# Retention's first two projections issued inside attention's last head, and its raw queries and keys read from other bank pairs

## The chip, the cores and the metric

The kernel runs on one core of a Trainium2 chip. Its time is the device time of one execution in microseconds (us). It is one program of 72862 instructions on five engines: PE (TensorE, matmuls), DVE (VectorE), ACT (ScalarE), POOL (GpSimd) and SP (SyncE, which issues the DMAs). Each engine runs its own instructions strictly in the order in which they are written; engines meet at semaphores only.

## The reference, cut to what matters

Two blocks follow each other on a sequence of 1024 tokens of width 1024. The second block has two layers, and the change is in both. Each layer is

```
h = rmsnorm(x); proj = h @ w_in                  # columns aq, ak, av, ag, bq, bk, bv, bg, cu, cg
o_a = diff_attention(aq, ak, av) * silu(ag)      # 4 heads, two softmax maps each, 8 query blocks of 128
o_b = retention(bq, bk, bv) * silu(bg)           # 4 heads, rotary on bq and bk first
o_c = multiscale_pool(cu) * silu(cg)
x   = x + concat(o_a, o_b, o_c) @ w_out
rotary(t): t1, t2 = halves of t; [t1*cos - t2*sin, t1*sin + t2*cos]
```

The first block (RG-LRU with HGRN2, then RWKV-7) is not touched.

## The kernel before

**Projections.** `h` lies turned in SBUF as two fp16 parts, `u_hi` and `u_lo`; the weights come in units of 1024 x 128, split into `w_hi` and `w_lo`, in a ring of four slots. A product is three matmuls (hi x hi, hi x lo, lo x hi) for each of eight tiles of 128 rows. `channel_major` (L128) gives 128 channels by 1024 tokens: 2 halves x 8 tiles x 3 = 48 matmuls of 128x512 into two PSUM banks. `token_major` (L148) gives the transposed form in 192 matmuls of 128x128. PSUM has 8 banks; `bank_pair(n)` is banks 2n and 2n+1. A slot's round is tracked by `stage_full` (weights landed), `w_half` and `w_full` (split), `w_free` (last matmul of the unit done; the same semaphore tells ACT that the unit's result may be read).

**Attention** (`diff_attention`, once for each layer) runs 32 steps `s`: four heads of eight query blocks. The order is written out by hand. In step `s` PE issues the logits of step `s+2` (12 matmuls, L2287, into banks 0 to 3), turns the attention map of step `s` in two halves (L2301, bank 4), multiplies it with the values in two halves (L2315, bank 5), and between these it issues four *pieces*: a quarter each of one half of a projection of the next head (L2259, L2265, banks 6 and 7). The last head, steps 24 to 31, has no next head, so its pieces are empty. DVE in step `s` adds the bias to the logits of `s+2` and takes their maximum (L2475, twice), combines the two maps of step `s+1` (L2485 to L2492), and then takes what the last piece left in PSUM (`low`, L2460 and L2465). ACT in step `s` first evicts the projection half of the step before (L2370 to L2379), copies the first turned half out (`take_turned`, L2390), does the two exponentials of `s+2` (L2384), and every fourth step takes the finished output (`take_values`, L2397 and L2398) before it copies the second turned half. A norm (L2325) follows on PE two steps behind, its tail (L2403 to L2506) on ACT and DVE. The semaphore `taken[half]` counts the projection halves that were taken out of bank 6 (half 0) or 7 (half 1); its sixteenth count belongs to the gate of the last head. For half 1 that is done in step 24, by ACT and then by DVE after `combine(25)`. POOL splits the weights of retention's four units in the last head; SP has loaded them before.

**Retention** is a block of its own behind it: all engines begin it together when the block before has ended on all. SP loads nine constants (L2612), then weights. PE projects units 0, 1, 2 (queries and keys of head pairs) into bank pairs 0, 1, 2; `cross(n)` (L2627, 2 fp32 matmuls, each two records in a profile) swaps the rotary halves of a raw tile; unit 3 goes to pair 3; `double(0)` (L2640), `cross(2)`, then the values of head 0 (L157). ACT begins with the softplus of twelve decay numbers (L314), which waits for a DVE operation behind the constants, and then, `take_raw` (L2728), evicts each unit and splits the high part of the next weights of that slot (L109). DVE finishes the softplus (L323 to L2789), splits low parts (L115) and rotates (L2799 to L2803, three operations for each raw tile).

Of the kernel before, what the change touches and what calls it, by code (L numbers as in the profile page):

```python
# [20 lines left out]
KT = D // P  # L21
TT = S // P
HALF = 512
# [107 lines left out]
def channel_major(pe, K, slot, rnd, u_hi, u_lo, banks, tile_ready=None):  # L131

    pe.wait_ge(K.w_full[slot], rnd + 2)
    w_hi = K.w_hi[:, slot, :].rearrange("p (k c) -> p k c", k=KT)
    w_lo = K.w_lo[:, slot, :].rearrange("p (k c) -> p k c", k=KT)
    for half, bank in enumerate(banks):
        cols = slice(half * HALF, (half + 1) * HALF)
        for k in range(KT):
            if half == 0 and tile_ready is not None:
                pe.wait_ge(tile_ready, k + 1)  # L140
            for n, (w, u) in enumerate(((w_hi, u_hi), (w_hi, u_lo), (w_lo, u_hi))):
                last = pe.matmul(K.psum[:, bank, :], w[:, k, :], u[:, k, cols],  # L142
                                 start=(k == 0 and n == 0), stop=(k == KT - 1 and n == 2))
    last.then_inc(K.w_free[slot], 1)


def token_major(pe, K, slot, rnd, u_hi, u_lo, banks):
# [163 lines left out]
def small_softplus_scalar(act, x_ready, y_ready, x, y):  # L311

    act.wait_ge(x_ready, 1)
    act.activation(y, x, ACT.Abs)  # L314
    act.drain()
    act.activation(y, y, ACT.Exp, scale=-1.0).then_inc(y_ready, 1)
# [1854 lines left out]
def diff_attention(nc, K, A, tag, layer, first_round, ahead):  # L2171

    H, NQ = A_HEADS, TT
    N = H * NQ
    lam_init = 0.8 - 0.6 * float(np.exp(-0.3 * layer))
    with nc.cleanup_on_exit(), ExitStack() as c:
# [6 lines left out]
        q, k = ([split(late_slots[n][:, a, :]) for n in range(2)] for a in range(2))  # L2183
# [25 lines left out]
        def unit_of(s):  # L2209

            h, j = divmod(s, NQ)
            return (h + 1, j // 2, j % 2) if 0 <= s and h + 1 < H else None
# [8 lines left out]
        with nc.Block() as block:  # L2221
# [21 lines left out]
            def _(pe):  # L2243
# [77 lines left out]
                def norm(part, s):  # L2321

                    pe.wait_ge(o_taken, part + 1)
                    pe.wait_ge(turned_ready, 2 * s + 2)
                    pe.matmul(K.psum[:, T_BANK, :], K.ones[:, :], sq[:, cols(part % 2)], start=True,  # L2325
                              stop=True).then_inc(norm_done, 1)

                def piece(s, n):
                    unit = unit_of(s)
                    if unit:  # L2330
                        project(*unit, n)

                whole(0)
                whole(1)
# [4 lines left out]
                for s in range(N):  # L2339
# [12 lines left out]
                    if part is not None:  # L2352
                        norm(part, s)
                values(N - 1, 1)
                norm(2 * H - 1, N - 1)

            @block.scalar
            def _(act):
# [188 lines left out]
def retention(nc, K, A, tag, layer, first_round, ahead):  # L2547
# [7 lines left out]
    H = B_HEADS  # L2555
    w_in = A["w_in_2"][layer].rearrange("(k p) c -> p k c", p=P)
    with nc.cleanup_on_exit(), ExitStack() as c:
# [37 lines left out]
        chunks = lambda x: x.rearrange("p (c t) -> p c t", c=TT)  # L2595
        cols = lambda half: slice(half * HALF, (half + 1) * HALF)

        SWAP_PAIR = (0, 1, 3, 3)
        slot_of = lambda hd, n: (2 * (hd % 2) + n, first_round + 1 + hd // 2)

        with nc.Block() as block:
# [16 lines left out]
            @block.tensor  # L2618
            def _(pe):
                def cross(n):  # L2620

                    i, a = divmod(n, 2)
                    pe.wait_ge(raw_ready, 4 if n == 2 else n + 1)
                    if n == 3:
                        pe.wait_ge(swap_taken, 3)
                    for half in range(2):
                        last = pe.matmul(K.psum[:, 2 * SWAP_PAIR[n] + half, :], swap[:, :],  # L2627
                                         rot[a][:, i, cols(half)], start=True, stop=True)
                    last.then_inc(swapped, 1)

                def double(hd):
                    i, b = divmod(hd, 2)
                    pe.wait_ge(rotated, 2 * i + 2)
                    if hd:
                        pe.wait_ge(scores_taken, hd)
                    else:
                        pe.wait_ge(raw_ready, 3)
                    for n in range(2):
                        for half in range(2):
                            last = pe.matmul(K.psum[:, 2 + 2 * n + half, :], twice[:, b, :],  # L2640
                                             rot[n][:, i, cols(half)], start=True, stop=True)
                        last.then_inc(doubled, 1)

                def values(hd):
                    if hd:
                        pe.wait_ge(g_taken, hd)
                    else:
                        pe.wait_ge(swap_taken, 1)
                    token_major(pe, K, *slot_of(hd, 0), K.u_hi, K.u_lo, (0, 1))

                def score(hd):
                    i, b = divmod(hd, 2)
                    rows = slice(64 * b, 64 * b + 64)
                    pe.wait_ge(qk2_ready, 2 * hd + 2)
                    for ch in range(TT):
                        toks = slice(ch * P, (ch + 1) * P)
                        last = pe.matmul(chunks(K.bank_pair(1))[:, ch, :], rot[1][rows, i, toks], rot[0][rows, i, toks],
                                         start=True, stop=True)
                    last.then_inc(scores_done, 1)

                def turn(hd):
                    for ch in range(TT):
                        last = pe.transpose(chunks(K.bank_pair(2))[:, ch, :], qk2[:, 1, ch * P:(ch + 1) * P],
                                            K.ident[:, :])
                    last.then_inc(k2_done, 1)

                def delta(hd):
                    pe.wait_ge(k2_ready, hd + 1)
                    pe.wait_ge(v_ready, hd + 1)
                    if hd:  # L2670
                        pe.wait_ge(norm_taken, hd)
                    else:
                        pe.wait_ge(swap_taken, 4)
                    for ch in range(TT):
                        last = pe.matmul(chunks(OUT)[:, ch, :], k2_turned[:, ch, :], v[:, ch, :],
                                         start=True, stop=True)
                    last.then_inc(delta_done, 1)

                def output(hd):
                    pe.wait_ge(scores_taken, hd + 1)  # L2680
                    pe.wait_ge(state_ready, hd + 1)
                    for ch in range(TT):
                        pe.matmul(chunks(OUT)[:, ch, :], v[:, ch, :], scores[:, ch, :], start=True, stop=False)
                        last = pe.matmul(chunks(OUT)[:, ch, :], state[:, ch, :], qk2[:, 0, ch * P:(ch + 1) * P],
                                         start=False, stop=True)
                    last.then_inc(out_done, 1)

                def norm(hd):
                    pe.wait_ge(o_taken, hd + 1)
                    for half in range(2):  # L2690
                        last = pe.matmul(K.psum[:, 6 + half, :], K.ones[:, :], sq[:, cols(half)],
                                         start=True, stop=True)
                    last.then_inc(norm_done, 1)

                for n in range(3):
                    channel_major(pe, K, n, first_round, K.u_hi, K.u_lo, (2 * n, 2 * n + 1))
                pe.wait_ge(consts_in, 16 * 9)
                cross(0)
                cross(1)
                channel_major(pe, K, 3, first_round, K.u_hi, K.u_lo, (6, 7))  # L2700
                for hd in range(H):
                    double(hd)
                    if hd == 0:
                        cross(2)
                    values(hd)
                    if hd:
                        norm(hd - 1)
                    score(hd)
                    turn(hd)
                    if hd == 0:  # L2710
                        cross(3)
                    delta(hd)
                    channel_major(pe, K, *slot_of(hd, 1), K.u_hi, K.u_lo, (0, 1))
                    output(hd)
                norm(H - 1)
# [5 lines left out]
            @block.scalar  # L2721
            def _(act):
                act.preload_act_table_set("natural_log_exp_and_others")
                small_softplus_scalar(act, logit_ready, y_ready, neg_logit[:, :], y[:, :])

                def take_raw(n):
                    unit_done(act, K, n, first_round)
                    act.mul(rot[n % 2][:, n // 2, :], K.bank_pair(n),  # L2728
                            UNSCALE * (KEY_SCALE if n % 2 else 1.0)).then_inc(raw_ready, 1)
                    split_high(act, K, n, first_round + 1)  # L2730

# [16 lines left out]
                    act.wait_ge(m_ready, hd + 1)  # L2748
                    act.mul(K.m_hi[:, hd + H, :], O[:, :], U_SCALE).then_inc(hi_ready, 1)

                for n in range(3):
                    take_raw(n)
                act.wait_ge(gamma_ready, 1)
                decays(0)
                take_raw(3)
# [416 lines left out]
```

## Time and profile before

| what | us |
|---|---|
| median of 3 runs | 3684.61 (3682.11 to 3686.03) |
| the profiled execution | 3681.23 |
| its span, first to last instruction | 3679.2 |
| first layer: attention's last head, then retention up to head 0's values | 2367.9 to 2429.5, to 2481.5 |
| second layer: the same | 3165.6 to 3227.6, to 3279.9 |

Times in rows are microseconds from the start of the span. The clock in a row is the mean granted TensorE clock of the stretch as a share of 2.4 GHz: 1.00 is that, 0.50 is 1.2 GHz.

### The profile page before, as it was taken

The numbers are of one execution on the slowest core, as the hardware profiler recorded it, in microseconds if no ns is written. First come the engines' busy times: TensorE is split into PE (matmuls) and PEld (weight loads), VectorE is DVE, ScalarE is ACT, GpSimd is POOL, SyncE is SP. The second block draws the span as 40 slices with busy tenths as digits, with TensorE's granted clock in tenths as the row PEclk, the third lists the DMA queues.
The fourth block names the chain that finished last, engine by engine and source line by source line (L and its number), as shares of the span: only waits on it lengthen the run. The fifth ranks groups of instructions, "written<-read, shape, count | busy, mean of one in ns | idle before, by whom it ended". The sixth has DMA issues, their size and how long they took to land. (4 is left out here: it accounts for less than half of the span.)

```text
span 3679.2 us, 72862 instructions
## 1 busy us (share of the span) xinstructions
PE 3348.3 (91%) x32106; PEld 2085.2 (57%) x32106; DVE 1877.1 (51%) x2548; ACT 1406.7 (38%) x2026; POOL 551.2 (15%) x350
## 2 busy tenths in 40 slices
PE   6987999978979898999998899989889999899889
PEld 3334666663434343999996466647434566657334
DVE  4654566662253833666663566644352366633442
ACT  3553444442354632333332445533211355523211
POOL 3000000002000001333331133200150232100330
PEclk9998999979989999999999999999999999999999
DMA  5101110104035643111113111020120211020211
GB/s 166 34 23 50 30 40 29 40 0 149 1 107 118 153 115 114 64 64 64 63 45 105 52 46 40 2 62 24 39 82 27 66 38 35 1 68 18 62 62 46
DMA packets 308329, 215.24 MB, mean 59 GB/s; under 512 B 125411, under 2 KB 283950, under 8 KB 305454
## 3 DMA queue, kind: packets, MB, share of 16 engines
q1 hardware_dynamic: 307608, 210.70, 19.2%
q8 instruction: 230, 3.77, 0.4%
q10 hardware_dynamic: 442, 0.37, 0.0%
q14 instruction: 49, 0.40, 0.0%
HBM read 173.26 MB, written 41.98 MB: 59 GB/s over the span
## 5 line engine op out<-in xcount | busy, mean ns | idle before, releaser
L142 PE MATMUL psum<-u,w_hi 128*128 128x512 f16 x2816 | 855.8, 386 | 103.1 <-DVEq L798 32.0
L142 PE MATMUL psum<-u,w_lo 128*128 128x512 f16 x1408 | 542.4, 385 | 0.0
L142 PEld LDWEIGHTS psum<-u,w_hi 128*128 128x128 f16 x2816 | 279.1, 100 | 452.4 <-issue 55.6
L97 POOL TENSOR_TENSOR w_hi<-stage,w_scale 128x1024 f16<-128x1024 f32 x52 | 99.4, 1912 | 1244.8 <-PE psum L142 600.0
L1063 PE MATMUL psum<-w_hi,merged 128*128 128x512 f16 x768 | 236.1, 389 | 24.9 <-PEq L2887 9.1
L115 DVE SCALAR_TENSOR_TENSOR w_lo<-stage,w_hi 128x1024 f16<-128x1024 f32 x124 | 149.3, 1220 | 186.1 <-ACT w_hi L109 186.0
L2475 DVE CUSTOM_DVE_ANT_0 probs_att<-psum,bias_att 128x1024 f32<-128x1024 f32 x128 | 156.8, 1225 | 167.8 <-PE psum L2287 167.6
L142 PEld LDWEIGHTS psum<-u,w_lo 128*128 128x128 f16 x1408 | 139.8, 99 | 172.8 <-issue 11.9
L2265 PE MATMUL psum<-u,w_hi 128*128 128x512 f16 x768 | 231.6, 383 | 6.3 <-PEq L966 6.3
L1063 PE MATMUL psum<-held_hi_out,merged 128*128 128x512 f16 x768 | 231.0, 379 | 0.0
L157 PE MATMUL psum<-w_hi,u 128*128 128x128 f16 x2048 | 173.2, 219 | 0.0
L157 PE MATMUL psum<-w_lo,u 128*128 128x128 f16 x1024 | 172.3, 219 | 0.0
L142 PE MATMUL psum<-mix_b_rp,w_hi 128*128 128x512 f16 x512 | 153.6, 382 | 11.9 <-DVE mix_b_rp L1569 11.4
L157 PEld LDWEIGHTS psum<-w_hi,u 128*128 128x128 f16 x2048 | 158.0, 98 | 4.9 <-issue 4.6
L2384 ACT ACTIVATE probs_att<-probs_att,neg_max_att 128x1024 f32<-128x1024 f32 x128 | 146.3, 1146 | 19.5 <-DVE neg_max_att L2479 19.4
L2315 PE MATMUL psum<-turned_att,merged 128*128 128x128 f32 x1024 | 139.7, 281 | 15.0 <-ACT sq_att L2398 14.6
L2099 DVE COPY_PREDICATED Tt_rc<-tmask_rc,psum 128x256 f32<-128x256 uint32 x192 | 83.6, 444 | 131.9 <-PE psum L1789 110.9
L1063 PE MATMUL psum<-w_lo,merged 128*128 128x512 f16 x384 | 149.4, 389 | 0.0
L2315 PEld LDWEIGHTS psum<-turned_att,merged 128*128 128x128 f32 x1024 | 132.2, 195 | 27.7 <-issue 17.7
L109 ACT ACTIVATE w_hi<-stage 128x1024 f16<-128x1024 f32 x124 | 127.6, 1048 | 53.2 <-PE psum L1063 42.3
L1063 PEld LDWEIGHTS psum<-w_hi,merged 128*128 128x128 f16 x768 | 76.6, 100 | 124.4 <-issue 38.3
L2265 PE MATMUL psum<-u,w_lo 128*128 128x512 f16 x384 | 146.9, 382 | 0.0
(444 smaller groups left out, 6804.8 us busy)
## 6 DMA issues: line engine op xcount, KB each, us to landing
stage<-w_in SPq DMA_DIRECT2D x72, 512.0 KB, 4.0
X<-rwkv_chunks SPq DMA_DIRECT2D x14, 1792.0 KB, 8.0
stage<-ab_w_in SPq DMA_DIRECT2D x48, 512.0 KB, 4.9
stage<-rw_w_in SPq DMA_DIRECT2D x32, 512.0 KB, 4.7
rwkv_chunks<-work_rp SPq DMA_DIRECT2D x26, 512.0 KB, 6.0
stage<-w_out SPq DMA_DIRECT2D x24, 512.0 KB, 5.5
X<-x SPq DMA_DIRECT2D x16, 512.0 KB, 10.7
stage<-ab_w_out SPq DMA_DIRECT2D x16, 512.0 KB, 6.4
```

What stands on the lines that cost most here:

```text
L97: pool.tensor_tensor(K.w_hi[:, slot, :], K.stage[:, slot, :], scale, ALU.mult).then_inc(K.w_half[slot], 1)
L109: act.mul(K.w_hi[:, slot, :], K.stage[:, slot, :], W_SCALE).then_inc(K.w_half[slot], 1)
L115: dve.scalar_tensor_tensor(K.w_lo[:, slot, :], K.stage[:, slot, :], W_SCALE, K.w_hi[:, slot, :], ALU.mult, ALU.subtract).then_inc(K.w_full ...
L142: last = pe.matmul(K.psum[:, bank, :], w[:, k, :], u[:, k, cols], start=(k == 0 and n == 0), stop=(k == KT - 1 and n == 2))
L157: last = pe.matmul(out, u[:, k, toks], w[:, k, :], start=(k == 0 and n == 0), stop=(k == KT - 1 and n == 2))
L1063: last = pe.matmul(bank_of(half, t), m[:, 2 * u + k, toks(t)], w[:, at, w_cols], start=(u == 0 and k == 0 and n == 0), stop=(u == UH - 1 a ...
L2099: dve.copy_predicated(Tt[:, q, g * GJ:g * GJ + GJ], mask, data).then_inc(t_ready, 1)
L2265: last = pe.matmul(K.psum[:, PROJ + half, :], w[:, kt, :], u[:, kt, cols(half)], start=(kt == 0 and n == 0), stop=(kt == KT - 1 and n == 2))
L2315: last = pe.matmul(K.psum[:, O_BANK, (i % 4) * P:(i % 4 + 1) * P], v_tiles[h % 2][:, half * 4 + n, :], turned[:, half, n, :], start=(half ...
L2384: act.activation(probs[:, s % 2, m, :], probs[:, s % 2, m, :], ACT.Exp, bias=neg_max[:, s % 2, m:m + 1], accum_out=sums[:, s % 2, m:m + 1] ...
L2475: dve.tensor_tensor_reduce(probs[:, s % 2, m, :], K.bank_pair(m), bias[:, h % 2, at:at + S], LOGIT_UNSCALE, LOWEST, ALU.add, ALU.max, neg_ ...
```

## The change

Attention's empty pieces are filled. Of retention's unit 0 (48 matmuls, now into banks 6 and 7) pieces 0 to 23 of the last head issue two matmuls each; of unit 1 (into banks 0 and 1) pieces 24 to 31 issue two each, then 8 follow behind the last values and 24 behind the last norm. Retention starts with unit 2. Its bank pairs change, ACT takes raw tiles 0 and 1 before the softplus, and `cross(2)` stands ahead of `double(0)`.

```diff
+UNIT_PRODUCTS = 2 * KT * 3
+def channel_part(pe, K, slot, rnd, u_hi, u_lo, banks, first, count):
+    if first == 0:
+        pe.wait_ge(K.w_full[slot], rnd + 2)
...
+    for i in range(first, first + count):
+        half, k, n = i // (KT * 3), i // 3 % KT, i % 3
...
+    if first + count == UNIT_PRODUCTS:
+        last.then_inc(K.w_free[slot], 1)
@@ diff_attention, PE
+                def next_stage(unit, first, count):
+                    if first == 0 and unit == 0:
+                        for half in range(2):
+                            pe.wait_ge(taken[half], 4 * H)
+                    elif first == 0:
+                        pe.wait_ge(logits_taken, 2 * N)
+                    channel_part(pe, K, unit, first_round + H, K.u_hi, K.u_lo, ((PROJ, PROJ + 1), (0, 1))[unit],
+                                 first, count)
                 def piece(s, n):
                     unit = unit_of(s)
+                    at = (s - (H - 1) * NQ) * 4 + n
                     if unit:
                         project(*unit, n)
+                    elif at < 24:
+                        next_stage(0, 2 * at, 2)
+                    else:
+                        next_stage(1, 2 * (at - 24), 2)
...
                 values(N - 1, 1)
+                next_stage(1, 16, 8)
                 norm(2 * H - 1, N - 1)
+                next_stage(1, 24, UNIT_PRODUCTS - 24)
@@ retention
-        SWAP_PAIR = (0, 1, 3, 3)
+        RAW_PAIR = (3, 0, 1, 2)
+        SWAP_PAIR = (3, 0, 3, 3)
@@ PE: cross, double(0), values(0)
-                    pe.wait_ge(raw_ready, 4 if n == 2 else n + 1)
-                    if n == 3:
+                    pe.wait_ge(raw_ready, n + 1)
+                    if n == 2:
+                        pe.wait_ge(swap_taken, 1)
+                    elif n == 3:
                         pe.wait_ge(swap_taken, 3)
-                        pe.wait_ge(raw_ready, 3)
+                        pe.wait_ge(raw_ready, 4)
-                        pe.wait_ge(swap_taken, 1)
+                        pe.wait_ge(swap_taken, 2)
-                for n in range(3):
-                    channel_major(pe, K, n, first_round, K.u_hi, K.u_lo, (2 * n, 2 * n + 1))
+                channel_major(pe, K, 2, first_round, K.u_hi, K.u_lo, (2, 3))
                 pe.wait_ge(consts_in, 16 * 9)
                 cross(0)
                 cross(1)
-                channel_major(pe, K, 3, first_round, K.u_hi, K.u_lo, (6, 7))
+                channel_major(pe, K, 3, first_round, K.u_hi, K.u_lo, (4, 5))
+                cross(2)
                 for hd in range(H):
                     double(hd)
-                    if hd == 0:
-                        cross(2)
                     values(hd)
@@ ACT
-                small_softplus_scalar(act, logit_ready, y_ready, neg_logit[:, :], y[:, :])
...
-                    act.mul(rot[n % 2][:, n // 2, :], K.bank_pair(n),
+                    act.mul(rot[n % 2][:, n // 2, :], K.bank_pair(RAW_PAIR[n]),
...
-                for n in range(3):
-                    take_raw(n)
+                take_raw(0)
+                take_raw(1)
+                small_softplus_scalar(act, logit_ready, y_ready, neg_logit[:, :], y[:, :])
+                take_raw(2)
```

## Rows read from the trace of the kernel before

**Rows 1.** The page's first part: busy time and share of the span, each engine.
```profile
PE 3348.3 (91%) x32106; PEld 2085.2 (57%) x32106; DVE 1877.1 (51%) x2548; ACT 1406.7 (38%) x2026; POOL 551.2 (15%) x350
```

**Rows 2.** Stretches, first layer: busy time of engines, granted clock, DMA share, GB/s.
```profile
2349.30:2368.00 18.70, 18.70 (x123) 11.25 (x124) 13.23 (x24) 13.53 (x20) 5.17 (x3) 1.00 0.00 1
2368.00:2429.50 61.50, 40.15 (x278) 28.31 (x278) 40.20 (x74) 34.15 (x58) 5.91 (x3) 0.89 0.00 1
...
2442.00:2452.30 10.30, 10.30 (x49) 4.70 (x48) 1.52 (x4) 1.97 (x2) 0.00 (x0) 1.00 0.36 97
...
2404.00:2408.00 4.00, 3.99 (x18) 2.50 (x20) 0.00 (x0) 0.34 (x1) 0.00 (x0) 0.50 0.02 4
```

**Rows 3.** Timeline of PE, step 24: start, duration, then the idle time before.
```profile
2367.93 1.47 PE L2287 MATMUL psum<-merged 64*128 64x512 f16 x12
2369.33 0.66 PE L2301 MATMUL psum<-ident,attn_att 128*128 128x128 f32 x4
...
2374.71 1.35 PE L2315 MATMUL psum<-turned_att,merged 128*128 128x128 f32 x8 [3.39 <-ACT sq_att L2398]
2375.99 2.74 PE L2287 MATMUL psum<-merged 64*128 64x512 f16 x12
```

**Rows 4.** Timeline of DVE, step 24: the sixteenth taking of bank 7.
```profile
2376.49 0.69 DVE L2465 SCALAR_TENSOR_TENSOR merged<-psum,merged 128x512 f32<-128x512 f32 x1
```

**Rows 5.** Timeline of ACT, step 24.
```profile
2370.02 0.59 ACT L2390 COPY turned_att<-psum 128x512 f32<-128x512 f32 x1
2370.95 1.15 ACT L2384 ACTIVATE probs_att<-probs_att,neg_max_att 128x1024 f32<-128x1024 f32 x1 [0.34 <-DVE neg_max_att L2479]
...
2373.97 0.60 ACT L2398 ACTIVATE sq_att<-psum 128x512 f32<-128x512 f32 x1
```

**Rows 6.** Timeline of the second layer: logits that end step 24, and bank 7's taking.
```profile
3173.42 1.47 PE L2287 MATMUL psum<-merged 64*128 64x512 f16 x12
...
3174.15 0.69 DVE L2465 SCALAR_TENSOR_TENSOR merged<-psum,merged 128x512 f32<-128x512 f32 x1
```

**Rows 7.** Waits, first layer's last head: who waited for whom, total, times, longest.
```profile
PE psum L2315 <- ACT sq_att L2398: 7.3, 2, 3.9
...
PE psum L2325 <- ACT turned_att L2390: 3.5, 2, 1.9
...
PE psum L2301 <- DVE attn_att L2492: 2.1, 2, 1.1
```

**Rows 8.** Timeline of PE: the last two steps, the last norm, retention's first matmuls.
```profile
2415.46 0.63 PE L2301 MATMUL psum<-ident,attn_att 128*128 128x128 f32 x4 [0.82 <-issue]
...
2419.98 2.00 PE L2315 MATMUL psum<-turned_att,merged 128*128 128x128 f32 x16
2423.15 1.12 PE L2325 MATMUL psum<-sq_att,ones 128*128 128x512 f32 x2 [1.17 <-ACT sq_att L2398]
2429.53 1.01 PE L142 MATMUL psum<-u,w_hi 128*128 128x512 f16 x2 [5.26 <-PEq L2176]
```

**Rows 9.** Timeline of DVE: its last operation in the attention block.
```profile
2427.96 0.69 DVE L2506 SCALAR_TENSOR_TENSOR merged<-O_att,merged 128x512 f16<-128x512 f32 x1 [0.70 <-ACT merged L2410]
```

**Rows 10.** Source line 71: retention's first two weight loads, issue and landing.
```profile
L71 SPq DMA_DIRECT2D stage<-w_in x2: 587/588/590, 2433.9 to 2434.5; - x2
...
DMA to landing us min/median/max: 5.2/5.8/6.4
```

**Rows 11.** Timeline of DVE and ACT, retention's start in the first layer.
```profile
2437.18 0.17 DVE L2785 TENSOR_SCALAR neg_logit_ret<-neg_logit_ret 128x12 f32<-128x12 f32 x1 [6.48 <-DMA neg_logit_ret<-ret_decay_logit]
...
2441.85 0.17 DVE L2789 TENSOR_SCALAR log_gamma_ret<-softp_ret 128x12 f32<-128x12 f32 x1
...
2442.95 1.05 ACT L109 ACTIVATE w_hi<-stage 128x1024 f16<-128x1024 f32 x1
...
2472.07 1.23 DVE L2803 TENSOR_TENSOR merged<-merged,crossed_ret 128x1024 f32<-128x1024 f32 x1
```

**Rows 12.** Timeline of PE: `double(0)`, behind the fourth unit.
```profile
2476.34 3.60 PE L2640 MATMUL psum<-merged,twice_ret 128*128 128x512 f32 x8
```

More of the change, by code:

```diff
@@ L144, in channel_major @@
     last.then_inc(K.w_free[slot], 1)
+UNIT_PRODUCTS = 2 * KT * 3
+def channel_part(pe, K, slot, rnd, u_hi, u_lo, banks, first, count):
+    if first == 0:
+        pe.wait_ge(K.w_full[slot], rnd + 2)
+    w_hi = K.w_hi[:, slot, :].rearrange("p (k c) -> p k c", k=KT)
+    w_lo = K.w_lo[:, slot, :].rearrange("p (k c) -> p k c", k=KT)
+    for i in range(first, first + count):
+        half, k, n = i // (KT * 3), i // 3 % KT, i % 3
+        w, u = ((w_hi, u_hi), (w_hi, u_lo), (w_lo, u_hi))[n]
+        last = pe.matmul(K.psum[:, banks[half], :], w[:, k, :], u[:, k, half * HALF:(half + 1) * HALF],
+                         start=(k == 0 and n == 0), stop=(k == KT - 1 and n == 2))
+    if first + count == UNIT_PRODUCTS:
+        last.then_inc(K.w_free[slot], 1)
 def token_major(pe, K, slot, rnd, u_hi, u_lo, banks):
```

## The prediction

> **What bounds the kernel now.** I read the page's busy shares first: PE has work in 91% of the span [rows 1], so a matmul is only saved, or hidden for nothing, where PE stands idle. The table of stretches shows where. In a head that still has projections PE is busy for 18.70 of 18.70 us; in attention's last head it is busy for 40.15 of 61.50 us, at a mean clock of 0.89 [rows 2]. So 21 us of PE time lie open there, in each of two layers. The waits say for whom PE stops: twice for ACT's `take_values` (7.3 us together), for turned copies and for DVE's combined map [rows 7]. Behind it, retention's start is a plain row of matmuls: one unit of 48 takes 10.3 us with PE always busy [rows 2]. That makes 0.215 us for each matmul at full clock, 0.43 for a piece of two.
>
> **What retention loses, step by step.** I count from retention's first instruction, R (2429.53 before [rows 8]). `double(0)` began at R + 46.8 [rows 12].
>
> New order on PE: unit 2 (R + 10.4), `cross(0)` and `cross(1)`. `double(0)` has 8 records that start every 0.43 us (3.44 us in all [rows 12]); a cross has 4, so 1.72 us: R + 13.8. Unit 3: R + 24.2. `cross(2)`: R + 25.9. Then `double(0)` needs both rotations, and here something else is late. ACT takes raw 0 at once but then waits for its next weights: they land at 2433.9 + 5.2, which is R + 9.6, the second at 2434.5 + 6.4, R + 11.4 [rows 10]. With 1.05 us for a high split [rows 11] ACT is free for the softplus at R + 12.5 (before: R + 7.9, just behind 2437.18). The softplus takes 4.6 us on both engines (from the end of DVE's first operation, 2437.35, to 2442.02, the end of its last [rows 11]): R + 17.1. DVE then has two small operations (0.35, estimate), three low splits at 1.2 and two rotations of three operations at 1.23 [rows 11]: 0.35 + 3.6 + 7.4 gives R + 28.4. So PE stands for 2.5 us and `double(0)` starts at R + 28.4, 18.4 earlier. `cross(2)` no longer follows it (1.72), so head 0's values come **20.1 us earlier after R**. The constants (landed by R + 7.7 [rows 11]) stay hidden behind unit 2. Unit 1's old cover for the softplus is gone, which is just those 2.5 us. Bounds: 17.5 (PE restarts at half clock after that stop), 21 (the rotations are ready when PE is, or nearly).
>
> **What attention gains in work.** SP and POOL get nothing new, no DMA moves, and the weights of units 0 and 1 are split before the head begins (POOL's three operations in it [rows 2] are for slot 3); so it is PE's order alone.
>
> *The new wait in step 24.* The first piece waits for both counts of 16. Bank 7's is DVE's `low` of step 24, which ended at 2376.49 + 0.69 = 2377.18 [rows 4]. The piece stands ahead of the turn that ran at 2369.33 [rows 3]. DVE's path to that point does not need this turn (logits of step 26 are issued ahead of the wait, the maps of step 25 are there), so DVE is no later, and no deadlock arises. But queued behind the wait are turn, values and logits of step 27, and behind the turn ACT's copy, two exponentials and `take_values`. Before, ACT took 4.55 us from the copy's start to the end of `take_values` (2370.02 to 2374.57 [rows 5]), of which 0.34 a wait that is over by then: 4.2. From 2377.2: piece and turn 0.9 at full clock, ACT 4.35 with latency, values 0.9, piece 0.43: logits(27) at 2377.2 + 6.6 = 2383.8. PE will have stood 7.8 us and restarts, I expect, at half clock, as after the 3.93 us stop, when the clock was 0.50 [rows 2]: piece and turn take 0.9 more. So 2384.7 against 2375.99 [rows 3]: **8.7 later**; in the second layer 3174.84 + 7.5 = 3182.3 against 3173.42 [rows 6]: 8.9. Bounds 7.8 and 9.8.
>
> *Steps 25 to 29.* Four pieces add 1.7 us of PE to a step. Cost zero: they lie in the stops for ACT (3.9), for turned copies (1.9) and for DVE's map (1.1) [rows 7], and where logits come up to 0.9 later they wait for DVE anyway. If a stop were not there, its pieces would cost 0.43 each. The clock goes both ways: logits took 2.74 instead of 1.47 us [rows 3]; with more work in between I take one such stretch fewer, minus 1.0, bounds minus 2.5 and plus 2.
>
> *Steps 30, 31 and the end.* PE ran without a stop from 2415.46 to 2422 [rows 8]. Seven pieces lie in it: +3.0. The next 8 matmuls (1.72) take the place of a 1.17 wait ahead of the norm: +0.55. The last 24 take 5.2 behind the norm's 0.86, against a tail on ACT and DVE of 5.5 (2423.15 to 2428.65 [rows 8, 9]): +0.6 with PE's latency. Together 4.2, bounds 3.5 and 7 (pieces at half clock).
>
> **Sum.** Attention later by 8.8 - 1.0 + 4.2 = 12.0 (9 to 15.5); retention shorter by 20.1 (17.5 to 21). The difference is -8.1, bounds -12 and -2; two layers: **-16**. The profiled execution took 3681.2; it would be 3665. The median shown is 3.4 above that, so 3684.6 - 16 = **3669**. Everything behind head 0's values keeps its waits, since it is timed from the same points.
>
> One page bears on the disputed clock. After the 5.26 us stop the first unit's matmuls ran slow [rows 8]; here row and page agree. The Trainium skill, page "TensorE: Matmul & The Clock Gate", section "HAM oscillation — how this bites in real kernels", says that every long stop is paid again in a slow restart, and its section "Part 4: PE-mode transpose" that transposes do not count as work for the clock. By these rules a head made of turns and a 7.8 us stop could stay slow; that is the third rival. No row here separates transposes from other matmuls.
>
> **Rivals.**
>
> 1. *The wait costs little.* If `low` came before the turn is due, or DVE used the stop to get ahead, the 8.8 would vanish: -16.9 a layer, 3651. Against: `low` ended 7.85 us behind the turn in the first layer [rows 3, 4], and DVE's next work needs logits that stand behind the wait.
>
> 2. *The retention start becomes bound by ACT and DVE.* If landings come 3 us later, each microsecond shows in full, since the chain landing, softplus, splits, rotations is already last by 2.5. With the attention at its upper end the two layers give back all: -1 to -3 each, 3680. For: the 2.5 us stop is no margin. Against: the loads are issued by the same SP order after R.
>
> 3. *Slower: the clock stays low in the last head.* PE's work for a step is 4.2 at full clock without pieces (18.70 / 2 [rows 2], less 24 matmuls of 0.215), 5.9 with them; at half clock 11.8, while steps 24 to 29 lasted 7.9 on average (2367.93 to 2415.46 in six [rows 3, 8]). Then PE is the bound: 3.9 more for each of five steps, and pieces and products of the end cost twice (+8): some 27 more a layer, 3720. It decides from about 8 us of loss, two such steps. Against: the low stretch after 3.93 us of standing ended within the next steps, and the mean was 0.89 [rows 2].
>
> The change is no empty one: order and waits of PE are new.
>
> **How the numbers follow.** Forecast 0.68 (own range 3662 to 3676), first rival 0.11, second 0.13, third 0.08. A measurement tells 0.2% or 7.4 us from no change. Faster: 0.68 + 0.11 = 0.79 (the own range lies beyond 7.4); same 0.13; slower 0.08. Range 3656 to 3680: it takes in the bounds of the sum (-24 to -4) and cuts most of the first rival and all of the third.
>
> **What would show it.** In step 24 the turn starts behind DVE's L2465, PE idle about 7.8 us, released by DVE. Logits(27) come 8 to 9 us later, while steps 25 to 29 keep their length. About 60 + 12 us from logits(26) to retention's first matmul. In retention `double(0)` starts at 28.4 behind R after a stop for DVE's rotation; its softplus starts near R + 12.5. Wrong it is if the stop in step 24 is under 5 us, if clocks of 0.5 fill more than a fifth of the head, or if `double(0)` starts before R + 26 or behind R + 31.

## The result, and the profile after

| | before | changed |
|---|---|---|
| median, first comparison (5 runs each) | 3682.11 | 3661.65 (3658.35 to 3665.21) |
| median, second comparison (7 and 4 runs) | 3682.78 | 3664.67 (3663.59 to 3666.59) |
| profiled execution, first | 3681.23 | 3658.40 |

The ratio is 0.9941 (95% interval 0.9926 to 0.9955), and 0.9953 (0.9937 to 0.9970) the second time: faster by 20.5 us the first time and 18.1 the second. The forecast was 3669, a fall of 16 from a median of 3684.61, with 0.79 for faster.

The stretches of the changed kernel, in the columns of [rows 2]: two steps with projections, the last head of the first and of the second layer, retention's first 10.3 us.

```profile
2353.50:2372.20 18.70, 18.70 (x123) 11.26 (x124) 13.22 (x24) 13.54 (x20) 5.21 (x3) 1.00 0.00 1
2372.20:2443.40 71.20, 58.33 (x376) 38.31 (x376) 40.20 (x74) 33.84 (x58) 5.91 (x3) 0.93 0.00 1
3156.70:3227.90 71.20, 58.46 (x376) 38.32 (x376) 40.20 (x74) 33.85 (x58) 5.91 (x3) 0.93 0.00 1
2443.40:2453.70 10.30, 10.30 (x48) 4.76 (x49) 1.09 (x2) 3.29 (x4) 0.00 (x0) 1.00 0.84 246
```

The head is 9.6 us longer (9.2 in the second layer) and holds 98 more matmul records (the two units are 96 matmuls; a few records can be missing) and 18 us more of PE work. Its mean clock is 0.93 instead of 0.89. Step 24 on PE, then DVE's taking of bank 7; they answer to [rows 3, 4]:

```profile
2372.17 1.47 PE L2305 MATMUL psum<-merged 64*128 64x512 f16 x12
2381.53 1.01 PE L159 MATMUL psum<-u,w_hi 128*128 128x512 f16 x2 [7.89 <-issue]
...
2388.89 1.47 PE L2305 MATMUL psum<-merged 64*128 64x512 f16 x12
...
2380.74 0.69 DVE L2499 SCALAR_TENSOR_TENSOR merged<-psum,merged 128x512 f32<-128x512 f32 x1
```

PE stands for 7.89 us and goes on 0.10 behind the end of DVE's operation (2381.43). The profile names no releaser ("issue"); DVE's row beside it points at the cause, and e1 and e2 below test it. From logits(26) to logits(27) it is 16.72 us, against 8.06. The clock of four stretches from the stop on:

```profile
2377.50:2381.50 4.00, 0.00 (x0) 0.00 (x1) 3.75 (x4) 0.00 (x0) 1.10 (x1) 0.50 0.00 0
2381.50:2385.50 4.00, 3.97 (x15) 3.08 (x16) 0.00 (x0) 2.07 (x4) 0.00 (x0) 0.50 0.00 0
2385.50:2389.50 4.00, 3.88 (x25) 2.58 (x25) 0.00 (x0) 2.23 (x5) 0.00 (x0) 0.84 0.00 0
2389.50:2436.00 46.50, 42.53 (x299) 29.42 (x296) 30.75 (x60) 25.66 (x44) 0.00 (x0) 1.00 0.00 1
```

The restart is at half clock. From 2389.50 to the end of the head it is full (1.00 from 2436.0 to 2443.4 too). The waits of the head, answering to [rows 7]:

```profile
PE psum L2333 <- ACT sq_att L2432: 2.9, 1, 2.9
...
PE psum L2343 <- ACT turned_att L2424: 0.6, 2, 0.3
```

One stop for `take_values` is left, that of step 28: 2.9 instead of 3.9. In step 24 ACT now does this work while PE, behind its 7.89 us stop, is busy at half clock. The stops for turned copies are 0.6 instead of 3.5. The end of the head, [rows 8, 9], and retention's start, [rows 11, 12]:

```profile
2436.31 1.02 PE L2343 MATMUL psum<-sq_att,ones 128*128 128x512 f32 x2
...
2443.40 0.59 PE L142 MATMUL psum<-u,w_hi 128*128 128x512 f16 x2 [0.89 <-PEq L2194]
...
2471.15 1.13 PE L2677 MATMUL psum<-merged,twice_ret 128*128 128x512 f32 x2 [1.73 <-DVE merged L2839]
```

```profile
2452.67 1.06 ACT L109 ACTIVATE w_hi<-stage 128x1024 f16<-128x1024 f32 x1 [7.00 <-DMA stage<-w_in]
...
2455.49 0.20 ACT L332 ACTIVATE y_ret<-neg_logit_ret 128x12 f32<-128x12 f32 x1
```

ACT's first high split waits 7.00 us for the weights, so the softplus starts at R + 12.1 and `double(0)` at R + 27.75, after PE has stood for 1.73 us. From logits(26) to `double(0)` it is 98.98 us in the first layer (2372.17 to 2471.15) against 108.41 [rows 3, 12]; with `cross(2)` already done (1.72) that is a gain of 11.2 us, and of 12.2 in the second layer. The sum, 23.3, is the difference of the two profiles (22.8) within 0.5: all other stages together give nothing.

### The profile page after: what moved, and what is told of

Read it like the earlier page. It is cut to its first block and busy times, and to the rows that moved or that the text cites. A ratio compares the mean times of both kernels' runs of the same rounds, so it can differ in the third digit from the quotient of the medians.

```text
span 3656.4 us, 72868 instructions
## 1 busy us (share of the span) xinstructions
PE 3338.5 (91%) x32106; PEld 2085.5 (57%) x32106; DVE 1876.7 (51%) x2548; ACT 1406.3 (38%) x2026; POOL 551.6 (15%) x350
## 5 line engine op out<-in xcount | busy, mean ns | idle before, releaser
L142 PE MATMUL psum<-u,w_hi 128*128 128x512 f16 x2688 | 815.0, 385 | 94.2 <-DVEq L816 32.0
L142 PE MATMUL psum<-u,w_lo 128*128 128x512 f16 x1344 | 516.4, 384 | 0.0
L142 PEld LDWEIGHTS psum<-u,w_hi 128*128 128x128 f16 x2688 | 265.9, 100 | 425.0 <-issue 42.9
L2283 PE MATMUL psum<-u,w_hi 128*128 128x512 f16 x768 | 231.5, 383 | 6.3 <-PEq L984 6.3
L142 PE MATMUL psum<-mix_b_rp,w_hi 128*128 128x512 f16 x512 | 153.7, 382 | 11.9 <-DVE mix_b_rp L1587 11.4
L2283 PE MATMUL psum<-u,w_lo 128*128 128x512 f16 x384 | 146.8, 382 | 0.0
L1081 PE MATMUL psum<-held_lo_out,merged 128*128 128x512 f16 x384 | 145.5, 379 | 0.0
```

The lines of the kernel that those rows point to most:

```text
L1081: last = pe.matmul(bank_of(half, t), m[:, 2 * u + k, toks(t)], w[:, at, w_cols], start=(u == 0 and k == 0 and n == 0), stop=(u == UH - 1 a ...
L2283: last = pe.matmul(K.psum[:, PROJ + half, :], w[:, kt, :], u[:, kt, cols(half)], start=(kt == 0 and n == 0), stop=(kt == KT - 1 and n == 2))
```

## The experiments

The theory under test: the change gains by hiding most of a layer's 96 moved matmuls in PE's stops; it pays 8.7 us a layer for one wait that is too strict, and the stop ahead of `double(0)` (1.73 and 1.47 here, 2.11 and 1.89 in a2_changed_again) for a softplus that has lost its cover.

**e1_half_waits**, the wait for each bank where that bank is first written.

```diff
-                    if first == 0 and unit == 0:
-                        for half in range(2):
-                            pe.wait_ge(taken[half], 4 * H)
+                    if unit == 0:
+                        if first % (KT * 3) == 0:
+                            pe.wait_ge(taken[first // (KT * 3)], 4 * H)
```

> The changed kernel, but the first piece of step 24 waits only for bank 6 (the gate's half 0, taken in step 23) and the wait for bank 7 stands where the first matmul of unit 0 goes into it, in step 27. Theory: the wait for DVE's step 24 is what costs 8.7 us a layer (logits(26) to logits(27) 16.7 instead of 8.1). Without it that distance is 8.2 to 8.6 in both layers, PE's stop of 7.9 is gone, a stop of about 3 for ACT's take_values comes back, and the time falls by 16 to 17: 3645. Rival: the stop is harmless because something else (DVE's 9 us of idle time, or the clock) gives it back later; then the time falls by less than 6. A third possibility: with the short stop the clock falls to half later in the head, as in the kernel before, and takes 3 us a layer back: 3651.

Measured: 3645.84 (3642.12 to 3649.46), ratio to before 0.9897 (0.9881 to 0.9914), 18.8 below a2_changed_again, the changed kernel measured beside it. Step 24 on PE:

```profile
2373.04 1.47 PE L2305 MATMUL psum<-merged 64*128 64x512 f16 x12
2374.88 0.60 PE L2319 MATMUL psum<-ident,attn_att 128*128 128x128 f32 x4
...
2379.82 1.13 PE L2333 MATMUL psum<-turned_att,merged 128*128 128x128 f32 x8 [2.14 <-ACT sq_att L2432]
2381.36 2.74 PE L2305 MATMUL psum<-merged 64*128 64x512 f16 x12
```

From logits(26) to logits(27) it is 8.32 us (8.27 in the second layer), and the stop for `take_values` is back, with 2.14 and not the 3 expected. So the wait is the cause. Part of it was given back, by the third possibility: half clock returned, with 2.74 for the logits, and the heads took 66.7 and 64.4 us where 8.4 less than 71.2 would be 62.8. In the profiles the edit gains 14.2 us (3649.46 against 3663.65), in the medians 18.8; the profiled execution was the slowest of its four.

**e2_wait_only**, the kernel before with the wait and nothing else.

```diff
                     if unit:
                         project(*unit, n)
+                    elif s == (H - 1) * NQ and n == 0:
+                        for half in range(2):
+                            pe.wait_ge(taken[half], 4 * H)
```

> The kernel before, with nothing but the new wait: in step 24 the empty first piece waits until banks 6 and 7 are both taken. Theory: slower by 8 to 9 us a layer through the stop alone, 16 to 18 in all: 3699. The logits of steps 25 to 29 keep half-clock stretches, since no pieces fill the stops: expected mean clock of the head 0.85 or less. If the changed kernel's steps 25 to 29 kept the full clock because of the long stop itself (and not of the pieces), the clock stays at 1.00 here from logits(27) on and the loss is only about 6 a layer, 12 in all. Rival that the wait costs nothing: within 3 of before.

Measured: 3698.63 (3697.26 to 3703.03), ratio 1.0048 (1.0031 to 1.0065), 15.9 slower. The two heads:

```profile
2366.80:2438.10 71.30, 44.03 (x280) 32.07 (x280) 40.19 (x74) 33.85 (x58) 5.91 (x3) 0.82 0.00 1
3173.90:3242.90 69.00, 42.60 (x282) 30.24 (x280) 40.18 (x74) 33.89 (x57) 5.91 (x3) 0.87 0.00 1
```

They are 9.7 and 7.0 us longer than before, at 0.82 and 0.87. (The second row starts 0.8 us ahead of its head; the head itself, 3174.69 to 3243.73, has 0.86.) The expected 0.85 or less was met in the first layer alone. Steps 25 to 28, from logits(27) to logits(31), took 30.25 and 29.99 here at clocks of 0.89 and 0.90, and 28.24 at 1.00 in the changed kernel (29.56 at 0.94 in one head of a2_changed_again): behind the same stop it is the pieces, not the stop, that hold the clock up. They do not do so every time. In e1, with pieces and without the long stop, these steps took 30.84 and 28.73 at 0.89 and 0.98, against 29.99 and 29.49 at 0.90 and 0.92 before.

**e4_softplus_first**, ACT's order at retention's start (`evict_raw` is `take_raw` without its high split).

```diff
-                take_raw(0)
-                take_raw(1)
+                evict_raw(0)
+                evict_raw(1)
                 small_softplus_scalar(act, logit_ready, y_ready, neg_logit[:, :], y[:, :])
+                split_high(act, K, 0, first_round + 1)
+                split_high(act, K, 1, first_round + 1)
                 take_raw(2)
```

> The changed kernel, with ACT's order at retention's start altered: raw tiles 0 and 1 are evicted, then the softplus, and only then the two high splits that wait for the weights' landing. Theory: the softplus starts 4.6 us earlier (R + 7.8 instead of R + 12.1), DVE's chain is free of it, the stop of 1.7 us ahead of double(0) goes; double(0) at R + 25.9 to 26.2 instead of R + 27.75, faster by 1.6 to 1.9 a layer, 3.5 in all. Rival: the third low split, bound by the landing of the third weights, is last, and less than half of the 1.7 goes.

Measured: 3653.24 (3651.60 to 3657.22), ratio 0.9919 (0.9903 to 0.9936). The start of `double(0)`:

```profile
2466.13 1.88 PE L2664 MATMUL psum<-merged,swap_ret 128*128 128x512 f32 x4
2467.84 3.60 PE L2677 MATMUL psum<-merged,twice_ret 128*128 128x512 f32 x8
```

PE no longer stops: `double(0)` starts at R + 25.87 in both layers, against 28.14 and 27.92 in a2_changed_again. That is 4.3 us. There the operation itself also ran at half clock in the first layer, behind the stop:

```profile
2470.11 5.40 PE L2677 MATMUL psum<-merged,twice_ret 128*128 128x512 f32 x8 [2.11 <-DVE merged L2839]
```

It took 5.40 us instead of 3.60, so the edit gains 6.1 us up to the end of `double(0)`, nearly all of the 6.4 by which the profiled executions differ (3657.22 and 3663.65); the heads are alike in both. The medians are 11.4 apart, and that rest is not explained; the profiled execution was the slowest of its four.

**a2_changed_again**, the measure for the three above (no edit).

> The changed kernel once more, as the measure for the others of this call: 3658 to 3665, its two changed stages as in its first profile (logits(26) to retention's first matmul 71.2 us in both layers, from there to double(0) 27.75).

Measured: 3664.67. The first head took 71.22, the second 73.83: one half-clock stretch in the heads, behind the stop of step 28.

```profile
3201.72 2.04 PE L2333 MATMUL psum<-turned_att,merged 128*128 128x128 f32 x8 [2.93 <-ACT sq_att L2432]
3204.55 2.74 PE L2305 MATMUL psum<-merged 64*128 64x512 f16 x12
```

So the changed kernel too can lose 2.6 us there; both heads of its first profile were free of it. `double(0)` was expected at R + 27.75 and came at 28.14 and 27.92.

**e3_order_only**, retention's new order and banks with attention's pieces empty.

```diff
-                    elif at < 24:
-                        next_stage(0, 2 * at, 2)
-                    else:
-                        next_stage(1, 2 * (at - 24), 2)
...
-                next_stage(1, 16, 8)
                 norm(2 * H - 1, N - 1)
-                next_stage(1, 24, UNIT_PRODUCTS - 24)
...
+                channel_major(pe, K, 0, first_round, K.u_hi, K.u_lo, (6, 7))
+                channel_major(pe, K, 1, first_round, K.u_hi, K.u_lo, (0, 1))
                 channel_major(pe, K, 2, first_round, K.u_hi, K.u_lo, (2, 3))
```

> The kernel before with retention's new order and bank pairs alone: attention's pieces are empty again and all four units are projected in retention. Theory: PE's work at retention's start is the same and ACT's and DVE's chain (softplus behind raw 1) has 20 us more cover than in the changed kernel, so R to head 0's values is 52 as before and the time within 4 of before. Rival: the later softplus shows (it begins near R + 24 instead of R + 8, its low splits and rotations end near R + 41) and costs; it could do so only if double(0), at R + 48.5 behind cross(2), were later than that: expected no.

Measured: 3682.92 (10 runs), ratio 0.9998 (0.9988 to 1.0007). `double(0)` came at R + 48.88, behind `cross(2)`: the order costs and gains nothing by itself.

**e6_unit0_only**, unit 1 given back to retention (e3's removals but for the first two lines, and only unit 1 put back).

> The changed kernel with unit 1 given back to retention: pieces 24 to 31 and the 32 products at the head's end are left out, retention starts with units 1 and 2. Theory: attention ends 4.0 earlier (seven pieces 3.0, products ahead of and behind the norm 1.2), retention is 10.4 longer by the unit and 1.7 to 2.1 shorter, as the softplus has its cover again: slower than the changed kernel by 4.3 to 4.6 a layer, about 9 in all, 3671 to 3673. Rival: at the end of the head PE's work hides nothing (ACT's and DVE's tail is waited for anyway, the clock falls meanwhile); then unit 1 gains nothing there and this kernel is as fast as the changed one.

Measured: 3668.78 (3663.82 to 3677.67), ratio 0.9963 (0.9953 to 0.9972): 4 to 7 us slower than the changed kernel's two medians, against 9 expected. In the profile the head ends 4.0 earlier, as expected, but R to `double(0)` is 38.9 and 39.1, which is 11.2 and 11.6 longer and not 8.5. Nearly 3 of that is the clock (units 1 and 2 take 23.4 and 23.6 us, where two at 10.3 would be 20.6), since without products beside the tail PE stands for 5.26 us:

```profile
2436.19 1.01 PE L142 MATMUL psum<-u,w_hi 128*128 128x512 f16 x2 [5.26 <-PEq L2194]
2437.42 1.06 PE L142 MATMUL psum<-u,w_hi 128*128 128x512 f16 x2
```

Unit 1 in the head gains, then, and the rival falls; how much stays open between 4 (medians) and 15 (the stretch in the profiles).

**e5_both**, e1 and e4 together.

> The two edits that helped, together: the wait for bank 7 moved to where bank 7 is first written, and the softplus ahead of the two high splits. If they are independent (one is in attention's step 24, the other at retention's start), the gains add: from the changed kernel -18.8 (measured alone) and -4 (double(0) came at R + 25.87 instead of 28.1 and 27.9 in the profiles), 3641 to 3643; the stand-alone median of the second edit was 11 lower than the changed kernel's, and if all of that was its own, 3635. If the stop and the softplus hid each other, it stays at 3646.

Measured: 3638.83 (3636.49 to 3642.17), ratio 0.9884 (0.9867 to 0.9900). Both heads took 64.4 us, and `double(0)` came at R + 25.87. The gain of both is 25.8 from a2_changed_again's median, between 23.1 (e1's 18.8 with e4's 4.3) and 30.2 (with e4's 11.4). So neither edit hides the other, and, as 3635 is not reached, not all of e4's 11 was its own.

**e7_early_values**, e5 and in the last head `take_values` ahead of the exponentials.

```diff
+                    part = part_after(s, 1)
+                    if part is not None and s >= (H - 1) * NQ:
+                        take_values(part)
                     if s + 2 < N:
                         exponentials(s + 2)
-                    part = part_after(s, 1)
-                    if part is not None:
+                    if part is not None and s < (H - 1) * NQ:
                         take_values(part)
```

> Both helpful edits, and in the last head ACT takes the finished output (take_values) ahead of the two exponentials instead of behind them. Theory: what is left of PE's stops in steps 24 and 28 (3.4 and 3 us) is ACT's exponentials standing ahead of take_values; PE gets to the next logits earlier by 2 in each, DVE is then the bound (6 us a step), so 1 to 3 a layer, and fewer half-clock stretches: 2 to 6 less than both edits. Rival: DVE is the bound in these steps already and the exponentials, 1.1 later, delay the second turned half and DVE's map: no gain or 1 to 2 slower.

Measured: 3629.91 (3622.13 to 3634.52), ratio 0.9850 (0.9832 to 0.9868), the fastest version.

```profile
2375.14 1.47 PE L2305 MATMUL psum<-merged 64*128 64x512 f16 x12
...
2380.17 1.13 PE L2333 MATMUL psum<-turned_att,merged 128*128 128x128 f32 x8 [0.40 <-ACT sq_att L2432]
2381.66 1.47 PE L2305 MATMUL psum<-merged 64*128 64x512 f16 x12
```

The stop in step 24 is 0.40, the step 6.53 in both layers instead of 8.68 and 8.27 in e5, and step 28 takes 6.5 instead of 9.1. Both heads took 59.65 us at a mean clock of 1.00, less than before (61.6) although they hold two units more. The gain, 4.75 a layer and 8.9 in the medians, lies above the expected ranges (1 to 3, and 2 to 6 in all); a part of it is that no half-clock stretch is left. The rival falls.

## Why the prediction was right, and where its sizes were off

- *The new wait*: right in place, cause and size. Logits(27) came 8.66 later (8.89 in the second layer; 8.7 and 8.9 forecast), PE's stop was 7.89 (7.8), the restart at half clock. e1 takes it away alone and e2 adds it alone. The first rival falls.
- *Steps 25 to 29*: the steps grew no longer, as forecast; no run separates what the pieces took from what the clock gave back. The clock term was mis-sized: forecast -1.0. Steps 25 to 28 took 28.24 against 29.99 and 29.49, which is -1.75 and -1.26, and logits(31) behind them ran at full clock too. The head as a whole is 9.6 and 9.2 longer, not 12.0.
- *The end*: forecast +4.2. From logits(31) to R 26.27 against 23.55 and 24.72, +2.7 and +1.5; the two old values hold half-clock stretches of 1.3 and more, which the forecast left out. e6 gives the stretch without unit 1's products, with logits(31) at full clock: 22.28. Against that the work costs 4.0, near the 4.2 forecast.
- *Retention*: R to `double(0)` 27.75 and 27.5 (28.4 forecast), head 0's values 20.7 and 21.2 earlier (20.1), softplus at R + 12.1 (12.5). The second rival needed landings 3 us later and did not come; what the landings cost is the stop of 1.5 to 2.1 us that e4 removes and that the forecast had in its sum.
- *The third rival*, a clock that stays low, is refuted: 1.00 from 2389.5 to 2436.0. The Trainium skill, page "TensorE: Matmul & The Clock Gate", section "HAM oscillation — how this bites in real kernels", says that a long stop is paid again in a slow restart; the half clock behind the stops of 7.89 and 5.26 us agrees. Its section "Part 4: PE-mode transpose" says that transposes do not count as work for the clock; no run here tested that by itself.

So in the profiles the terms add to -11.0 and -12.1 us instead of -8.1. The step that was off is the clock term: with the end's old half-clock stretches it was 2.2 and 2.9 us too small. Retention's 0.6 and 1.1 are the rest. The medians fell by less than the profiles (18.1 and 20.5 against 22.8), and so came nearer to the forecast than the working did. One reason is on record: a2_changed_again lost 2.6 us in its second head and 1.8 in its first `double(0)` to half clock. Of the distance from 3669 to 3661.65, 2.5 us is the median before, which was 3682.11 here and 3684.61 in the sum.

One bound was added up wrongly. Attention's upper bound was given as 15.5, but its three terms' bounds (9.8, 2 and 7) add to 18.8; the largest measured is 11.8, a2_changed_again's second head.

## What to carry to other kernels

When work is filled into another stage's stops, give each piece only the wait for the buffer that it writes first: with the wait moved (e1) the change was worth 36.9 us, and the wait for both halves at the first piece took 18.8 of them. Look at what the removed work used to cover on the other engines (here a softplus behind a DMA), and put waits on transfers behind short work that others need. Fill can also hold the clock up, so look for half-clock stretches in the old stage and count them as possible gain, not as certain: behind the restart they were absent in both heads of the changed kernel's first profile, back in e1, and absent again in e7, where the stops themselves were short.

## What the runs showed of the hardware that was not expected

Behind a stop of 2.93 us in the same step 28 the matmuls ran at full clock in three heads of the changed kernel's profiles and at half in one (logits 1.47 or 2.74 us), which made that head 2.6 us longer. Over all versions that keep this stop (changed, a2, e1, e4, e5, e6) the logits behind it were slow in five heads of twelve. Shorter stops were followed by half clock too: 2.14 us in e1's first head, and 2.11 ahead of a2's first `double(0)`, while e1's second head kept full clock behind its 2.14. So the length of the stop alone did not decide. A stop of 7.89 or 5.26 was followed by half clock every time that it was seen.
